# Score steps in pairs in the attention stage of a two-layer fp32 trunk: a new order on TensorE, VectorE and ScalarE

## The reference

```python
def diff_attn_block(q, qpos, k, v, kpos, lam):
    s = jnp.einsum('bqhcd,bkhcd->bhcqk', q, k).astype(jnp.float32) * (DIFF_HD ** -0.5)
    visible = (kpos // CHUNK)[None, :] <= (qpos // CHUNK)[:, None]
    s = jnp.where(visible, s, -jnp.inf)
    p = jax.nn.softmax(s, axis=-1)
    a = p[:, :, 0] - lam * p[:, :, 1]
    return jnp.einsum('bhqk,bkhe->bqhe', a.astype(v.dtype), v)
```

## Time and profile before

| what | value |
|---|---|
| median of 3 runs | 2164.8 us (2164.68 to 2165.1) |
| profiled execution, own time | 2164.79 us |
| its span, first to last instruction | 2163.0 us |
| TensorE busy | 2147.8 us, 99% |
| VectorE, ScalarE, GpSimd busy | 56%, 45%, 40% |
| granted TensorE clock | 1.0 in the whole span |
| matmuls | 17696 |

### The profile page before, as it was taken

How to read it: one execution, slowest core, us unless ns; L and a number is a source line. 1 busy time by engine, 2 the same in 40 slices (tenths; PEclk the granted TensorE clock), 3 DMA queues, 4 the chain that set the end, 5 groups by cost and what they waited for, 6 DMA issues and landing times.

```text
span 2163.0 us, 43436 instructions
## 1 busy us (share of the span) xinstructions
PE 2147.8 (99%) x17696; PEld 2081.0 (96%) x17696; DVE 1213.6 (56%) x2107; ACT 975.1 (45%) x1882; POOL 872.0 (40%) x386
## 2 busy tenths in 40 slices
PE   7999999999999999999999999999999999999999
PEld 7899989999999999999998899999999999999999
DVE  6676666556355662266267676755563566623551
ACT  5655554445323452344246655544542335423441
POOL 4344423234443433433463354323443444334433
PEclk9999999999999999999999999999999999999999
DMA  5323222222222222221323233222222222222223
GB/s 176 100 85 106 79 86 87 72 94 81 79 86 91 82 83 82 98 98 61 107 94 100 73 107 100 72 72 85 83 80 97 78 84 93 80 88 98 90 68 111
DMA packets 76405, 193.71 MB, mean 90 GB/s; under 512 B 7760, under 2 KB 28848, under 8 KB 76208
## 3 DMA queue, kind: packets, MB, share of 16 engines
q1 hardware_dynamic: 67712, 184.51, 26.0%
q10 hardware_dynamic: 8496, 6.44, 0.9%
HBM read 177.50 MB, written 13.42 MB: 88 GB/s over the span
## 4 chain that ended last, share of the span: by engine, by line
PE 97%; DVE 2%; ACT 1%; DMA 0%; issue 0%; DVEq 0%; ACTq 0%
PE ps L654 13%; PE ps L656 13%; PE ps L655 13%; PE ps L703 7%; PE ps L704 7%; PE ps L705 7%; PE ps L1077 4%; PE ps L1076 4%; PE ps L1078 4%; PE ps L682 2%; PE ps L840 2%; PE ps L726 2%; PE ps L808 2%; PE ps L800 2%; PE ps L874 2%; PE ps L801 1%
## 5 line engine op out<-in xcount | busy, mean ns | idle before, releaser
L519 POOL TENSOR_TENSOR wlo<-raw,whi 128x1024 fp32r<-128x1024 f32 (+1 forms) x328 | 770.7, 2371 | 1010.5 <-ACT whi L1140 1010.5
L654 PE MATMUL ps<-hl,whi 128*128 128x272 f32 x2432 | 703.0, 289 | 0.0
L656 PE MATMUL ps<-hl,wlo 128*128 128x272 f32 x2432 | 701.0, 288 | 0.0
L655 PE MATMUL ps<-hl,whi 128*128 128x272 f32 x2432 | 699.7, 288 | 0.0
L654 PEld LDWEIGHTS ps<-hl,whi 128*128 128x128 f32 x2432 | 458.7, 189 | 0.0
L656 PEld LDWEIGHTS ps<-hl,wlo 128*128 128x128 f32 x2432 | 457.4, 188 | 0.0
L655 PEld LDWEIGHTS ps<-hl,whi 128*128 128x128 f32 x2432 | 457.1, 188 | 0.0
L1140 ACT ACTIVATE whi<-raw 128x1024 fp32r<-128x1024 f32 (+1 forms) x330 | 313.4, 998 | 203.9 <-PE ps L1078 179.3
L703 PE MATMUL ps<-whi,hl 128*128 128x256 f32 x1216 | 347.0, 285 | 0.0
L704 PE MATMUL ps<-wlo,hl 128*128 128x256 f32 x1216 | 343.0, 282 | 0.0
L705 PE MATMUL ps<-whi,hl 128*128 128x256 f32 x1216 | 342.6, 282 | 0.0
(11 more groups left out here) (241 smaller groups left out, 3325.9 us busy)
## 6 DMA issues: line engine op xcount, KB each, us to landing
raw<-in_w_units_dram SPq DMA_DIRECT2D x260, 512.0 KB, 4.7
raw<-in_w_down_units_dram SPq DMA_DIRECT2D x64, 352.0 KB, 3.4
kcT<-in_cache_k_dram SPq DMA_DIRECT2D x16, 256.0 KB, 2.9
out_new_k_prompt_dram<-rawk SPq DMA_DIRECT2D x8, 512.0 KB, 3.0
out_new_v_prompt_dram<-vd SPq DMA_DIRECT2D x8, 512.0 KB, 3.6
raw<-in_w_first_dram SPq DMA_DIRECT2D x6, 512.0 KB, 4.7
vc_n<-in_cache_v_dram SPq DMA_DIRECT2D x8, 256.0 KB, 4.2
vc_n<-in_cache_v_dram ACTq DMA_DIRECT2D x8, 256.0 KB, 2.7
```

Of the source, the lines that this page charges most:

```text
L519: e.tensor_tensor(wlo[:, s, a:b], raw[:, s, a:b], whi[:, s, a:b].bitcast(F32), ALU.subtract).then_inc(*S.up("w_ready", ("lo", j, part)))
L654: e.matmul(out, wh, hi, start=(c == 0), stop=False)
L655: e.matmul(out, wh, lo, start=False, stop=False)
L656: ins = e.matmul(out, wl, hi, start=False, stop=(c == KC - 1))
```

## The change

TensorE gets a new order of steps, in which scores stand in pairs. With the same names it is: F(4) S0 S1, F(7) W0, S2 S3, F(3) W1 V0, F(3) S4 W2 V1, F(3) W3 V2, S5 S6, F(6) W4 V3, F(3) W5 V4, S7 S8, F(6) W6 V5, F(2) S9 W7 V6, F(3) W8 V7, F(1) W9 V8, F(3) V9. With these shares the queries' sample tile is the first chunk behind S3. Three chunks more go ahead of the key transposes (`FILL_FIRST` of 21 in place of 18), and three fewer behind them.

VectorE's order becomes M0 M1, C0, C1 M2 M3, C2, C3 M4 SS, C4 M5 M6, C5, C6 M7 OS M8, C7 M9, C8, C9. On ScalarE the copies `hi("D", 4, 0)` and `hi("D", 4, 1)` move behind T3 and T4, one each. Nothing else changes: the instructions are the same in number and shape.

```diff
+                    def step(n, chunks):
+                        fill(chunks)
+                        weighted(n)
+                        if n:
+                            values(n - 1)
+
                     fill(2 * FILL_MID)
                     scores(0)
                     scores(1)
-                    for n in range(10):
-                        if n == 0:
-                            fill(FILL_SHARE[n])
-                        if n + 2 < 10:
-                            scores(n + 2)
-                        if n:
-                            fill(FILL_SHARE[n])
-                        weighted(n)
-                        if n:
-                            values(n - 1)
+                    step(0, FILL_SHARE[0])
+                    scores(2)
+                    scores(3)
+                    step(1, FILL_SHARE[1])
+                    fill(FILL_SHARE[2])
+                    scores(4)
+                    step(2, 0)
+                    step(3, FILL_SHARE[3])
+                    scores(5)
+                    scores(6)
+                    step(4, FILL_SHARE[4])
+                    step(5, FILL_SHARE[5])
+                    scores(7)
+                    scores(8)
+                    step(6, FILL_SHARE[6])
+                    fill(FILL_SHARE[7])
+                    scores(9)
+                    step(7, 0)
+                    step(8, FILL_SHARE[8])
+                    step(9, FILL_SHARE[9])
                     fill(len(FILL) - filled[0])
                     values(9)
...
-        FILL_FIRST = 18
+        FILL_FIRST = 21
         FILL_MID = 2
-        FILL_SHARE = (5, 4, 2, 6, 4, 5, 5, 4, 4, 1)
+        FILL_SHARE = (7, 3, 3, 3, 6, 3, 6, 2, 3, 1)
+        MAXES_BEHIND = {1: (2, 3), 3: (4,), 4: (5, 6), 6: (7, 8), 7: (9,)}
...
-                                if tt == 3:
-                                    hi("D", 4, 0)
-                                    hi("D", 4, 1)
...
                         take_filled(n)
                         turn(n)
+                        if n in (3, 4):
+                            hi("D", 4, n - 3)
                         if n:
                             out(n - 1)
...
                         combine(n)
-                        if n == NT + 2:
-                            e.wait_ge(*S.at("act_free_o", ("o", NT)))
-                            sum_of_sample(2 * p, "dve_free_o", "osum")
-                        if n + 2 < 10:
-                            maxes(n + 2)
-                        if ("s", 0) in filled_at(n - 1):
+                        for k in MAXES_BEHIND.get(n, ()):
+                            maxes(k)
+                            if k == 7:
+                                e.wait_ge(*S.at("act_free_o", ("o", NT)))
+                                sum_of_sample(2 * p, "dve_free_o", "osum")
+                        if n == 3:
                             e.wait_ge(*S.at("s_ready", ("q", 1)))
                             sample_sum(rawq[0:DEC, NT, :], "mm1", ("N", 3, 4), "q'")
```

## The result

The changed kernel took 2169.29 us (median of 14 executions, 2169.03 to 2170.43), the kernel before 2164.94 us (14 executions, 2164.2 to 2165.99) beside it: a ratio of 1.0021, 95% interval 1.0013 to 1.0028. It is slower by 4.4 us. The forecast was +4.8 us, 2169.6. The granted clock is 1.0, and TensorE's 17696 matmuls are the same in number and shape.

What follows compares the result with a forecast made beforehand. TensorE, at 99% of the span, was taken as the bound, with other engines' chains nearly as long. Following those chains, each body grows 0.6 us; eight give +4.8 on 2164.8, so 2169.6 us; range 2164 to 2173.

Steps and rivals of the forecast that it cites:

- two chains of dependences: Other engines' work from S2 to q1 and W4 to W8: 10.3 and 12.7 us, against TensorE's 9.7 and 11.2.
- Part 1, pairing: TensorE's scores in pairs save 0.6 to 1.5 us a body, taken as 1.5; 5 to 12 us over eight.
- the 0.4 for the rest: Estimated saving a body where S2, W0, S3 switched around one transpose and the sample tile shares S3's way out.
- The 0.38 a visit: Saving per visit to the scores avoided, from a range of 0.19 to 0.4; three visits fewer give 1.1 us.
- Part 2, the chunks: Three chunks moved ahead of the key transposes take 1.13 us of cover from the score steps, at no own cost.
- Part 3, the waits: New TensorE waits in each body: 0.6 us from S2 to q1, about 1.5 from W4 to W8.
- The wait at V4: One place of the 1.5 us lost from W4 to W8: V4 waits because O3 is late behind `hi`.
- The hold of C6: GpSimd's `lo` holds VectorE's second instruction of C6 until `lo` ends, costing 0.44 us a body.
- Rival 2: C6 is not held: 0.44 us less a body, 2166.2 us, called no change; chance 0.18.
- The late copy: ScalarE's second `hi`, 1.05 us, stands behind T4; O3, X6 and all behind them wait for it.
- Rival 1: Faster: the cover suffices, no waits come, only the pairing saving is left; 2153 to 2156 us; chance 0.12.
- Rival 3: Much slower: six waits a body each cost a 0.1 us restart, 4.8 us more, 2174.4 us; chance 0.10.

Runs made afterwards that it cites:

- experiment 7: Changed kernel with 18 chunks ahead of the key transposes, new shares, M4 behind C2, second `hi` behind T5: 2155.36 us, 0.9956 of the kernel before.
- 9: As experiment 7, with shares (7, 3, 1, 8, 0, 4, 6, 3, 6, 2) and the `hi` copies behind T5 and T6: 2154.89 us.
- experiment 5: Kernel before, old order, with 21 chunks ahead, new shares, `hi` copies behind T3 and T4, SS kept behind M5: 2164.92 us, 0.9999.
- experiment 3: Changed kernel with the three chunks moved back behind S0 (`FILL_FIRST` 18): 2161.41 us, 7.9 us less than the changed kernel.
- experiment 2: Changed kernel with only GpSimd's second `lo` made to wait for C6: 2166.15 us, 3.1 us less than the changed kernel.
- experiment 1: Changed kernel with the second `hi` behind T5 in place of T4: 2163.63 us, 5.7 us less than the changed kernel.
- 11: As experiment 10, but GpSimd waits for C7 before the second `lo`: 2155.57 us, 0.9958 of the kernel before.
- 12: Shares of experiment 10, with the `hi` copies behind T3 and T5 in place of T5 and T6: 2156.15 us, 0.996.
- experiment 10: As 9, with 17 chunks ahead of the key transposes and shares (8, 4, 0, 8, 0, 5, 5, 5, 5, 1): 2166.52 us, 1.0008.

## Why the prediction was right

The sum followed two chains of dependences, and the places at which they come out can be laid beside the trace (us from S0, fourth body):

| place | predicted | measured |
|---|---|---|
| q1 starts, behind SS | 14.11 | 14.11 |
| W4 starts | 16.36 | 16.33 |
| C6 ends | 21.56 | 21.49 |
| W8 starts | 29.10 | 28.93 |
| score steps end | 33.96 | 33.85 |
| body longer by | 0.6 | 0.57 |

**Part 1, pairing.** A pair of 256 keys takes 0.91 as said. The saving of 1.5 us a body was too high: 34.43 before, and 34.98 after (33.85 + 1.13) less some 1.9 of waits, make 1.35; without any wait experiment 7 gives 1.19. The term that was too high is the 0.4 for the rest: S2 W0 S3 took 1.87 before and W0 S2 S3 take 1.62 now, 0.25. The 0.38 a visit fits, but not by its parts, and that is luck. The first chunk behind a score costs hardly more than one behind a value product (12 matmuls take 1.53 behind S6, 1.52 behind V6). The step in costs more than the 0.1 taken. In the kernel before, V2 and V7 are the same six matmuls, the first ahead of a score, the second ahead of a chunk:

```profile
286.66 0.83 PE L874 MATMUL ps<-vd,aT 128*128 128x128 f32 x6
287.43 0.63 PE L840 MATMUL ps<-kdT,qdT 64*128 64x256 f32 x6
...
303.05 0.83 PE L874 MATMUL ps<-vd,aT 128*128 128x128 f32 x6
303.64 0.36 PE L808 MATMUL ps<-whi,hl 128*128 128x256 f32 x1
```

From start to next start they take 0.77 and 0.59: 0.18 for the step in, 0.19 for the block alone and 0.01 for the step out make 0.38. Two losses were not in the sum of the later orders: where the sample tile stands directly behind V0 and ahead of S4, as in experiments 7 and 9, V0's block is 0.32 in place of 0.14 and S4's 1.10 in place of 1.00. The rule of the Trainium skill (TensorEngine Tiling (Array Packing), Key Properties) that a switch of mode drains the engine is borne out as to its sign; its price is the 1.19 measured for three visits fewer and one direct passage more. No row shows the drain itself. In the changed kernel the waits take more than this away.

**Part 2, the chunks.** "No cost of its own" holds: experiment 5 moves them in the old order at no cost. But they were the cover. Laid back they give 7.9 us in the new order (experiment 3).

**Part 3, the waits.** Predicted were 2.1 us a body, 0.6 up to q1 and 1.5 from W4 to W8. Found are 0.53 up to q1 (0.12 at W3 for C3, 0.41 at q1 for SS) and about 1.4 behind it. They stand at V5 with W6 (0.3), W7 (0.76) and W8 (0.33). The wait at V4 that I named did not come: V4 started at 294.81, 0.08 after O3 ended (294.36 + 0.37), and from W5 to V4 are 0.20, as in experiment 7. Saving and waits were both forecast too high, 1.5 for 1.35 and 2.1 for 1.9. That leaves the forecast alone: the sum runs along the chain of the waits, in which the saving does not stand.

**The hold of C6** is shown. It is 0.42 for 0.44, the ends agree to 0.01 us, and taking it away alone gives 3.1 us. Rival 2, no hold, gave 2166.2, though its own 0.2 x 8 makes 2166.4; experiment 2 makes that case and measures 2166.15.

**The late copy.** "O3, X6 and all behind them wait for it" is shown by experiment 1, which frees both the copy's 1.05 us and the hold. The prediction said that the cover hides 11.2 of a chain of 12.7 from W4 to W8; with the copy elsewhere the wait at W7 falls from 0.76 to 0.13 (S9 to W7, 1.13 against 1.00).

**The rivals.** Rival 1 (the cover suffices) fell for this kernel, by 1.9 us of waits a body, and came true with other shares: experiments 7, 9, 11 and 12 lie at 2154.9 to 2156.2, in or beside its 2153 to 2156. Rival 3 (each wait costs a restart) fell: W7 started 0.05 after C7 ended, W8 0.06 after C8 (304.64, 304.70), and the blocks of W7 and V6 behind the wait are 0.38 and 0.37 where experiment 7, without a wait, has 0.36 and 0.37. The blocks of W3, W8 and V5 are 0.05 to 0.07 longer than without a wait, less than the rival's 0.1 and at three places, not six. I had charged 0.14 from the earlier trace rows; the 0.08 less at W8 and the 0.07 by which C6 ended earlier are most of the difference of 0.17 in the table's W8. At q1 it was 0.15 (L1764 ended 289.73), as charged.

**What stays open.** Why the last instruction of experiment 10 ended 0.42 after `lo` and not 0.62 is not told by any row; it may have done part of its work before it was held. The profile has no row for the hold itself: it shows as a long duration and as ends that meet.

## What to carry to other kernels

When a stream on the busiest engine is made cheaper, lay the dependent chain of the other engines beside it, piece by piece from the trace, before the edit: here 1.2 to 1.35 us a body were saved and 1.9 lost again, because two chains were 0.5 and 1.4 us longer than the cover left over them. A busy share tells nothing of this; 45% and 56% hid a copy of 1.05 us at a place that cost 5.7 us. And a move on an engine that is off the path is judged by what runs beside it afterwards: the same two `hi` cost nothing in one order and 6 us in another, and the mend was another share-out of the filling work, with the copies placed to suit it, which made the paired order 0.46% faster than the kernel before.

## What the runs showed of the hardware

- A `scalar_tensor_tensor` of VectorE that starts while GpSimd's subtraction of 128x1024 runs does not finish before it: 0.22 became 0.44 to 1.91 us for one element a partition, and 0.62 became 2.69 for 384. The same goes for `tensor_tensor`. In the 14 traces 1510 instructions of these two kinds with both tensors in SBUF start inside such a subtraction, and none ends before it; 4492 with one tensor in PSUM start inside one, and none is more than 0.03 us longer than the shortest of its line and shape. Instructions of VectorE that read PSUM kept their length beside a `lo`: M7's maximum took 0.96 without one, and 0.96 in experiment 10 beside one (293.83, the `lo` from 293.45 to 295.84). So did C6's reciprocal, with one input (0.17, right ahead of the held L1914).
- Which comes first decides, and closely: begun 0.08 us behind `lo`, VectorE lost 2.07 us; begun 0.22 us ahead, it lost none and `lo` took 0.24 longer. The Trainium skill (SBUF — State Buffer, SBUF: two separate sides) says that whichever starts first has the port for its whole instruction. These two rows agree, in both directions.
- A wait on TensorE of up to some 0.3 us leaves no mark of its own, since the record ahead of it is still open. The waits listed sum to 0.88 us a body, the start-to-start gaps to 1.9.
- A matmul starts 0.05 to 0.06 us after the end of the VectorE instruction that it waited for at W7 and W8, 0.15 after it at q1, and 0.14 at the transposes of stage M. No run shows what makes the difference.
